# One program instead of three blocks, another routing chain, and register values read ahead of the expert tiles

## The chip, the cores and the metric

The kernel runs on one core of a Trainium2 chip. A core has five engines with a queue of their own: TensorE (PE, matrix products; its weight loads are shown as PEld), VectorE (DVE), ScalarE (ACT), GpSimd (POOL) and SyncE (SP, here only for DMA transfers). They wait for one another by semaphores. The metric is the device time of one execution in microseconds, as a median of runs.

## What is computed

One layer of a decoder trunk over 1024 prompt tokens and 64 sample tokens (8 sequences of 8), each of width 1024. Token mixing and cross-attention come first; the change concerns the third part, a mixture of 16 experts in 4 groups of 4, of which each token uses two of one group:

```
def hierarchical_moe(h, w_group, b_group, w_router, b_router, w_gate, w_up, w_down):
    g_logits = (t @ w_group).astype(jnp.float32) + b_group.astype(jnp.float32)
    g_prob = jax.nn.softmax(g_logits, axis=-1)
    g_idx = jnp.argmax(g_logits, axis=-1)
    g_p = jnp.max(g_prob, axis=-1, keepdims=True)
    ...
    top_v, top_i = lax.top_k(e_sel, TOP_K_INNER)
    top_w = jax.nn.softmax(top_v, axis=-1) * g_p
    ...
    hg = jnp.einsum('td,edf->tef', t, w_gate)
    hu = jnp.einsum('td,edf->tef', t, w_up)
    a = jax.nn.silu(hg) * hu * gates[..., None].astype(t.dtype)
    y = jnp.einsum('tef,efd->td', a, w_down)
```

A root-mean-square norm with gain `g_ffn` stands ahead of it, a residual sum behind it, and a final norm behind that. An expert has a hidden width of 256.

## The kernel before

The tokens lie in nine tiles of 128 rows (`NT = 9`; tiles 0 to 7 are the prompt, tile 8, `TS`, holds the 64 sample rows and padding). Products that need f32 accuracy are made of three products of a high and a low part (`split_product`, L1503 to L1508); the high part is a rounding on ScalarE, the low part (`Wl`, `xTl`, `aTl`, `pTl`) a subtraction on VectorE.

The program consists of three blocks with a barrier of all engines between them.

Block 1 is mixing (`front_stage`) and attention (`attention_stage`). In the attention's last loop over tiles t, PE makes the scores of tile t+1, turns the probabilities of tile t (`turn_probs`) and multiplies them with the folded values (`out`, two halves of 24 products); DVE adds the result to the residual `X` (L995) and counts up `x2_ok`.

Block 2 is `routing_block` (L1202). For each of the nine tiles ScalarE sums squares (L1291), GpSimd makes the factor (L1280, L1283), DVE scales the row (`r_xs`, L1366), PE turns it by eight transposes (L1338), ScalarE copies the turned tile (`r_hT`, L1305), and PE makes 20 logits, 4 for groups and 16 for experts (L1324, L1325), which are copied and turned once more (`r_lgT`, L1295, L1329). SP stores the scaled rows in `h_rows` (three buffers), loads the first three experts' weights (nine transfers of 1 MB, `raw`) and stores `X` in `acc_rows`. Then a chain on DVE follows, in which nearly every step waits for the one before by `step_ok`: it picks the group (`G1`) and the two experts (`H`), makes the gate weights (`wt`), 0/1 rows for each token and choice (`M`, and their sum `Ms`), and has PE count how many tokens of each expert come earlier, within a tile (`before`) and in each tile as a whole (`ones`). From the counts DVE makes each choice's slot: running sums over the tiles (`run`, L1427), tiles per expert and first tile (`tl`, `base`), the slot's tile and row (`rk`, `bk`, `fl`, `rr`, `tt`). It builds one-hot matrices for the row (`r_big`, 18 x 128 columns, L1454) and the tile (`r_A`, with token numbers in one half and weights in the other, L1457 to L1462); 18 products on PE (L1354) turn them into a table of token numbers and of gate values for up to 32 tiles of slots. Meanwhile DVE makes tables for the engines' registers (`TAB`: does an expert start at this tile, where its weights lie, the last tile of each; L1467 to L1489). At the end it writes `idx` (L1496), `gate` and `idx_last`.

Block 3 is `experts_block` (L1512). `tile_steps` goes over the tiles of 128 slots; from the 18th on each is inside a condition, and with these inputs 27 tiles run. For each one GpSimd gathers rows of `h_rows` into `xg` (L1618) and of `acc_rows` into a ring (L1630), PE turns the rows (L1776), ScalarE and DVE split them (L1688, L1728), PE makes gate and up (`gate_up`, 24 products), ScalarE the silu (L1701), DVE the product with the gate value (L1740), PE turns that (`turn_a`, L1798) and multiplies it with the down weights (`down`, 12 products), DVE adds (L1748), GpSimd scatters (L1637). The weights of an expert are three pieces (`raw`, 128 x 2048 each), split at the tile where the expert starts (L1682 on ScalarE, L1723 on DVE). The engines read what they need from `TAB` into registers (`value_load`: `starts` L1551, `started` L1555, `place` L1559, `end` L1563, `tail` L1567, `sums` L1571, `last_slot` L1577). Behind the last tile PE reads two more values and does the last `down`; DVE reads four and adds (L1760); GpSimd waits for the scatter before (L1657) and for that sum (L1659) and issues the last scatter. Then the nine tiles are loaded from `acc_rows`, normed and stored.

## Time and profile before

| | us |
|---|---|
| median of 3 runs (1052.6 to 1054.3) | 1053.1 |
| the profiled execution's own time | 1054.8 |
| its span, first to last instruction | 1053.1 |
| PE busy | 940.9 (89%) |
| PE weight loads busy | 761.5 (72%) |
| DVE busy | 443.0 (42%) |
| ACT busy | 339.7 (32%) |
| POOL busy | 172.5 (16%) |

The profile is one execution seen by the hardware profiler. Times count from its first instruction. Busy shares of the whole span say little here, since the stages have different limits; the rows below are of stretches. An entry in square brackets behind a row is the time that the engine stood idle before it and what it waited for.

### The profile page before, as it was taken

To read this page: it belongs to the slowest core of one execution; us is meant where nothing else is said; L and a number is where in the kernel's file an instruction comes from. 1 tells how busy PE (TensorE), PEld (TensorE's weight loads), DVE (VectorE), ACT (ScalarE), POOL (GpSimd) and SP (SyncE) were. 2 spreads that over 40 slices of the span, in tenths; PEclk is the share of its full clock that TensorE was granted. 3 is DMA by queue.
4 is the path that set the end of the run, shared out by engine and by line. 5 is a ranking of instruction groups with operands and counts; after the bars stand their busy time and mean duration, and the time that the engine had idled before them with its cause. 6 is when DMAs were issued, how large, how long until landed. Compare 5 with 4: busy or idle time off the path is not lost. (4 is left out here: it accounts for less than half of the span.)

```text
span 1053.1 us, 14135 instructions
## 1 busy us (share of the span) xinstructions
PE 940.9 (89%) x4765; PEld 761.5 (72%) x4765; DVE 443.0 (42%) x565; ACT 339.7 (32%) x489; POOL 172.5 (16%) x188
## 2 busy tenths in 40 slices
PE   6996999999999999898999999763798999999960
PEld 5785888888888686466888887653587878787750
DVE  5673212212122124322322222437677786756724
ACT  6762012120121114122221211520555464444403
POOL 0011000000000000000100000400224453534511
PEclk9998999999999999998999999885799999999985
DMA  9892101111013985620000100793378888776328
GB/s 375 354 298 72 47 4 40 40 41 41 1 40 156 367 346 221 260 100 1 1 1 1 31 1 0 251 338 131 95 275 310 324 309 324 255 285 245 119 66 349
DMA packets 41391, 171.47 MB, mean 163 GB/s; under 512 B 8779, under 2 KB 13259, under 8 KB 30810
## 3 DMA queue, kind: packets, MB, share of 16 engines
q1 hardware_dynamic: 29266, 143.16, 36.1%
q0 software_dynamic: 12048, 27.32, 7.4%
q8 instruction: 44, 0.72, 0.3%
q14 instruction: 33, 0.27, 0.1%
HBM read 149.18 MB, written 37.63 MB: 177 GB/s over the span
## 5 line engine op out<-in xcount | busy, mean ns | idle before, releaser
L1723 DVE TENSOR_TENSOR Wl<-raw,Wh x48 | 109.4, 2289 | 64.6 <-ACT Wh L1682 64.6
L1682 ACT CAST Wh<-raw x48 | 91.1, 1910 | 73.6 <-issue 71.7
L1506 PE MATMUL ps<-Wh,e_xTh 128*128 x216 | 87.7, 406 | 7.1 <-issue 5.2
L558 PE MATMUL ps<-f_win_h,f_hTh 128*128 128x512 f32 x216 | 85.9, 398 | 0.6 <-DVE f_hTl L450 0.6
L1508 PE MATMUL ps<-Wh,e_xTl 128*128 x216 | 84.8, 392 | 0.0
L1507 PE MATMUL ps<-Wl,e_xTh 128*128 x216 | 84.8, 392 | 0.0
L560 PE MATMUL ps<-f_win_l,f_hTh 128*128 128x512 f32 x216 | 84.3, 390 | 0.0
L559 PE MATMUL ps<-f_win_h,f_hTl 128*128 128x512 f32 x216 | 84.1, 389 | 0.0
L1637 POOL DMA_INDIRECT acc_rows<-x,idx x26 | 46.6, 1793 | 118.2 <-DVE x L1748 47.6
L1506 PE MATMUL ps<-f_rg_h,f_cTh 128*128 128x512 f32 x144 | 56.7, 394 | 0.0
L1508 PE MATMUL ps<-f_rg_h,f_cTl 128*128 128x512 f32 x144 | 56.2, 390 | 0.0
L1507 PE MATMUL ps<-f_rg_l,f_cTh 128*128 128x512 f32 x144 | 56.1, 390 | 0.0
L1506 PEld LDWEIGHTS ps<-Wh,e_xTh 128*128 128x128 f32 x216 | 40.9, 189 | 19.5 <-issue 11.7
L1506 PE MATMUL ps<-t_WKh,t_hTh 128*128 128x512 f32 x128 | 51.8, 405 | 3.3 <-DVE t_hTl L940 3.3
L1506 PE MATMUL ps<-t_VWh,t_pTh 128*128 128x512 f32 x128 | 50.4, 394 | 2.4 <-DVE t_pTl L984 2.4
L1507 PE MATMUL ps<-t_WKl,t_hTh 128*128 128x512 f32 x128 | 50.9, 397 | 0.0
L1508 PE MATMUL ps<-t_WKh,t_hTl 128*128 128x512 f32 x128 | 50.8, 397 | 0.0
L1507 PE MATMUL ps<-t_VWl,t_pTh 128*128 128x512 f32 x128 | 49.8, 389 | 0.0
L1508 PE MATMUL ps<-t_VWh,t_pTl 128*128 128x512 f32 x128 | 49.8, 389 | 0.0
L517 DVE TENSOR_TENSOR f_xin<-f_xin,ps 128x512 f32<-128x512 f32 x18 | 12.4, 688 | 86.8 <-PE ps L1508 86.8
L267 POOL TENSOR_SCALAR f_st<-f_st 128x1 f32<-128x1 f32 x20 | 4.4, 219 | 270.5 <-ACT f_junk L347 223.3
L1508 PEld LDWEIGHTS ps<-Wh,e_xTl 128*128 128x128 f32 x216 | 40.8, 189 | 8.8
(315 smaller groups left out, 1899.7 us busy)
## 6 DMA issues: line engine op xcount, KB each, us to landing
raw<-in_w_e SPq DMA_DIRECT2D x48, 1024.0 KB, 8.5
t_ring<-in_kc SPq DMA_DIRECT2D x8, 1024.0 KB, 12.3
t_ring<-in_vc SPq DMA_DIRECT2D x8, 1024.0 KB, 8.4
f_win_raw<-in_w_in SPq DMA_DIRECT2D x3, 2048.0 KB, 23.6
f_xin<-in_x SPq DMA_DIRECT2D x9, 512.0 KB, 3.5
x_rows<-f_xin SPq DMA_DIRECT2D x9, 512.0 KB, 2.6
h_rows<-r_xs SPq DMA_DIRECT2D x9, 512.0 KB, 7.7
acc_rows<-x SPq DMA_DIRECT2D x9, 512.0 KB, 13.8
```

Source lines behind the costliest of these rows:

```text
L267: pool.tensor_scalar(st[:, c + 1:c + 2], st[:, c:c + 1], 1.0 / width, EPS, ALU.mult, ALU.add).then_inc(ok, 1)
L517: dve.tensor_tensor(half, half, ps[:, 7 if h == 0 else 5, :], ALU.add).then_inc(x1_ok, 1)
L558: pe.matmul(ps[:, bank, :], hTh[:, c, :], win_h[i][:, c, :], start=(c == 0), stop=False)
L559: pe.matmul(ps[:, bank, :], hTl[:, c, :], win_h[i][:, c, :], start=False, stop=False)
L560: last = pe.matmul(ps[:, bank, :], hTh[:, c, :], win_l[i][:, c, :], start=False, stop=(c == KC - 1))
L1506: pe.matmul(out, xh, wh, start=(n == 0), stop=False)
L1507: pe.matmul(out, xh, wl, start=False, stop=False)
L1508: last = pe.matmul(out, xl, wh, start=False, stop=(n == len(pairs) - 1))
L1637: pool.indirect_dma_start(acc_dram[:, :], bass.IndirectOffsetOnAxis(ap=IDX[:, j:j + 1], axis=0), ring[:, j % 4, :], None, bounds_check=NT ...
L1682: act.copy(Wh[q][:, ds(off, PIECE)], raw[q][:, ds(off, PIECE)]).then_inc(hi_ok[q], 1)
L1723: dve.tensor_tensor(Wl[q][:, ds(off, PIECE)], raw[q][:, ds(off, PIECE)], Wh[q][:, ds(off, PIECE)].bitcast(F32), ALU.subtract).then_inc(lo_ ...
```

## The change

The three blocks become one. `routing_block` is now `routing_stage` and `experts_block` `experts_stage`; both return one program for each engine, which `build` calls behind the attention's. No barrier stands between them; semaphores on single buffers do (`h_st`, `idx_ok`, `routed`, `x2_ok`, `out_ps`, `sc_ps`). The tiles are routed in the order 8, 0, 1, ..., 7 (`ORD`).

Into the attention's last steps go: three sums of squares on ScalarE, the scaling of the first three tiles on DVE, and on PE the turn of the first one. In SP's queue six weight pieces start when the last scores are done, three when the last product is done, and then the nine stores of `X`. The scaled rows are stored from ScalarE's queue. The scaled rows lie in `xg`, which isn't cleared any more.

The chain: logits are read from PSUM directly; the gate weights are computed behind the index; the counts come from ten bf16 products that sum up over earlier tiles (and give the totals in one more group of 16 columns); a slot's position is one number (`pos`), of which the tile is taken by adding and subtracting 1.5 x 2^23; `A` and the one-hot rows are bf16, the latter written by 18 instructions, each releasing one of 18 bf16 products that give the index. The gate values are 18 f32 products of their own (`G`). The register tables are made behind that, in `dve_tables`.

In the experts: ScalarE rounds the first expert's three pieces inside the routing program, DVE subtracts two of them ahead of the tables and the third behind; PE does tile 0 without registers and turns tile 1 behind tile 0's gate and up; DVE reads its four values for the end ahead of the tiles, PE its two in tile 1.

```
+            if t == TS - 1:
+                turn_scaled(pe, 0)
             for n in range(2):
                 out(t, n)
...
+            if t == TS - 1:
+                scaled(dve, 0)
+                scaled(dve, 1)
+            if t == TS:
+                scaled(dve, 2)
             if t >= 1:
                 for h in range(2):
                     dve.wait_ge(out_ps, 2 * (t - 1) + h + 1)
...
+        sp.wait_ge(A_["sc_ps"], 2 * TS)
+        for n in range(RING):
+            for p in (1, 2):
+                if n:
+                    sp.wait_ge(keep["w_ld"][p], 16 * n)
+                load_piece(sp, io, keep, n, p)
+        sp.wait_ge(A_["out_ps"], 2 * TS)
+        for n in range(RING):
+            if n:
+                sp.wait_ge(keep["w_ld"][0], 16 * n)
+            load_piece(sp, io, keep, n, 0)
+        for n, t in enumerate(ORD):
+            sp.wait_ge(A_["x2_ok"], 2 * n + 1)
+            sp.dma_start(acc_dram[t * P:(t + 1) * P, :], X[:, t, :]).then_inc(keep["acc_st"], 16)
...
+            act.copy(hT[n % 2][:, :, :], ps[:, BT(n), :].rearrange("p b (c t) -> p (b c) t", t=P)).then_inc(hT_ok, 1)
+            act.wait_ge(xs_ok, n + 1)
+            act.dma_start(h_dram[ORD[n] * P:(ORD[n] + 1) * P, :], xs[:, n % XG, :]).then_inc(h_st[n % XG], 16)
...
+        pe.matmul(ps[:, 6, 0:(NT + 1) * NE], before_b[:, :], Ms[:, :, :].rearrange("p t e -> p (t e)"), start=True, stop=False)
+        for n in range(NT):
+            last = pe.matmul(ps[:, 6, (n + 1) * NE:(NT + 1) * NE].rearrange("p (t e) -> p t e", e=NE), ones_b[:, :],
+                             Ms[:, n:n + 1, :].to_broadcast([P, NT - n, NE]), start=False, stop=(n == NT - 1))
+        last.then_inc(cnt_ps, 1)
+        pe.wait_ge(nA_ok, 1)
+        pe.wait_ge(pA_ok, 1)
+        for i in range(K2):
+            pe.wait_ge(big_ok, i + 1)
+            last = pe.matmul(ps[:, 7, 0:2 * NTILE].rearrange("p (a n) -> p a n", a=2), big_b[:, i, :], An[:, :, i, :],
+                             start=(i == 0), stop=(i == K2 - 1))
+        last.then_inc(idx_ps, 1)
+        pe.wait_ge(bigf_ok, 1)
+        pe.wait_ge(G_ok, 1)
+        for i in range(K2):
+            last = pe.matmul(ps[:, 4, 0:NTILE], big[:, i, :], G[:, i, :], start=(i == 0), stop=(i == K2 - 1))
+        last.then_inc(gate_ps, 1)
...
+        then(dve.scalar_tensor_tensor(out=R[:, :, :], in0=base_.rearrange("p (o e) -> p o e", o=1).to_broadcast([P, NT, NE]),
+                                      scalar=float(P), in1=rank, op0=ALU.mult, op1=ALU.add))
+        for k in range(2):
+            last = v(MR[:, k, :, 0:NE], M[:, k, :, :], R[:, :, :], ALU.mult)
+        then(last)
+        then(r(pos[:, :], MR[:, :, :, :].rearrange("p k t e -> p (k t) e"), AX_X, ALU.add))
+
+        then(dve.tensor_scalar(ta[:, :], pos[:, :], 0.5 - P / 2, 1.0 / P, ALU.add, ALU.mult))
+        then(dve.tensor_scalar(tb[:, :], ta[:, :], WHOLE, None, ALU.add))
+        then(dve.tensor_scalar(tile[:, :], tb[:, :], -WHOLE, None, ALU.add))
...
+        for i in range(K2):
+            dve.tensor_scalar(big_b[:, i, :], irow_b[:, :], rr[:, i:i + 1], None, ALU.is_equal).then_inc(big_ok, 1)
...
+        rest_of_first(0)
+        rest_of_first(1)
+        rest_of_xT(0, 0)
+        tables(dve)
+        rest_of_first(2)
+        rest_of_piece(1, (0, 1))
...
+        slot, landed, done_by = last_slot(dve), sums(dve, 0), [tail(dve, 1 + h) for h in range(2)]
+        tile_steps(dve, step)
-            tile_steps(dve, step)
-
-            slot, landed, done_by = last_slot(dve), sums(dve, 0), [tail(dve, 1 + h) for h in range(2)]
...
+            gate_up(s, like, *own(s))
+            if s == 0:
+                turn(1, 1)
...
+        last_end = []
+
+        def step_and_end(s, like):
+            step(s, like)
+            if s == 1:
+                last_end.extend((end(pe, NE - 1), tail(pe, 0)))
+        tile_steps(pe, step_and_end)
+        down(NTILE - 1, NE, (NE - 1) % RING * PIECE, last_end[0], [last_end[1]] * 2)
-            tile_steps(pe, step)
-            down(NTILE - 1, NE, (NE - 1) % RING * PIECE, end(pe, NE - 1), [tail(pe, 0)] * 2)
```

In PE's queue the end of the attention and the start of the routing read as follows. `t_VWh` are folded values, `t_E` probabilities, `r_xs` scaled rows (now in `xg`). Before:

```order
L1507 MATMUL ps<-t_VWl_133,t_pTh 128x512
L1508 MATMUL ps<-t_VWh_125,t_pTl 128x512
L1852 UNCONDITIONAL_BRANCH
L1315 UNCONDITIONAL_BRANCH [waits barrier_Pool_Activation_PE_DVE_SP_release]
L1338 MATMUL ps<-ident,r_xs 128x128 [waits r_xs_ok,r_ones_ok,r_c_ld]
L1338 MATMUL ps<-ident,r_xs 128x128 x7
```

and now, first at the turn of the last probabilities, then behind the last product:

```order
L1116 MATMUL ps<-ident,t_E 128x128 [waits t_pT_ok,t_p_ok]
L1116 MATMUL ps<-ident,t_E 128x128 x7
L1375 MATMUL ps<-ident,xg 128x128 [waits r_xs_ok]
L1375 MATMUL ps<-ident,xg 128x128 x7
L1586 MATMUL ps<-t_VWh_127,t_pTh 128x512 [waits t_x2_ok,t_pT_ok]
...
L1588 MATMUL ps<-t_VWh_134,t_pTl 128x512
L1375 MATMUL ps<-ident,xg 128x128 [waits r_xs_ok,r_ones_ok,r_c_ld]
L1375 MATMUL ps<-ident,xg 128x128 x7
L1389 MATMUL ps<-r_hT_157,r_wr 20x128 [waits f_hT_ok]
```

The first turn has moved ahead of the last product of the attention, and the barrier between them is gone. PE's queue from the index product to the first expert tile was, with `r_A` and `r_big` the one-hot matrices:

```order
L1354 MATMUL ps<-r_A,r_big 128x64 [waits r_AB_ok]
L1354 MATMUL ps<-r_A,r_big 128x64 x17
L1204 UNCONDITIONAL_BRANCH
L1769 UNCONDITIONAL_BRANCH [waits barrier_Pool_Activation_PE_DVE_SP_release]
L1776 MATMUL ps<-ident,xg 128x128 [waits e_x_ld0]
L1776 MATMUL ps<-ident,xg 128x128 x7
L1776 MATMUL ps<-ident,xg 128x128 [waits e_xT_ok,e_x_ld1]
L1776 MATMUL ps<-ident,xg 128x128 x7
```

and is now (`r_An` index, `r_G` gate values), up to tile 0's products and then behind them:

```order
L1418 MATMUL ps<-r_An,r_big_b 128x64 [waits r_big_ok,r_pA_ok,r_nA_ok]
L1418 MATMUL ps<-r_An,r_big_b 128x64 [waits r_big_ok] x17
L1424 MATMUL ps<-r_G,r_big 128x32 [waits r_G_ok,r_bigf_ok]
L1424 MATMUL ps<-r_G,r_big 128x32 x17
L1862 MATMUL ps<-ident,xg 128x128 [waits e_x_ld0]
L1862 MATMUL ps<-ident,xg 128x128 x7
L1586 MATMUL ps<-Wh_63,e_xTh_211 128x512 [waits e_lo_ok1,e_lo_ok0,e_xT_ok]
...
L1862 MATMUL ps<-ident,xg 128x128 [waits e_xT_ok,e_x_ld1]
L1862 MATMUL ps<-ident,xg 128x128 x7
L1884 MATMUL ps<-ident,e_sg 128x128 [waits e_a_ok]
```

A second set of products stands ahead of the first turn, and the turn of tile 1 has moved behind tile 0's gate and up. At PE's end, behind the turn of the last gated tile (`e_sg`), stood:

```order
L1581 UNCONDITIONAL_BRANCH
L1563 TENSOR_LOAD tab
L1563 ISA x2
L1567 TENSOR_LOAD tab
L1567 ISA x2
L1506 MATMUL ps<-Wh_4716,e_aTh 128x512 [waits e_y_ok,e_lo_ok2,e_aT_ok]
```

and stands now:

```order
L1884 MATMUL ps<-ident,e_sg 128x128
L1659 UNCONDITIONAL_BRANCH
L1586 MATMUL ps<-Wh_65,e_aTh 128x512 [waits e_y_ok,e_lo_ok2,e_aT_ok]
L1587 MATMUL ps<-Wl_68,e_aTh 128x512
L1588 MATMUL ps<-Wh_65,e_aTl 128x512
```

The two loads have left the place behind the branch.

## Rows read from the trace of the kernel before

**Rows 1.** Windows: busy us of each engine (instructions), clock, DMA share, GB/s
```profile
756.50:1012.50 256.00, 246.74 (x1188) 202.32 (x1188) 182.30 (x175) 126.18 (x123) 106.13 (x73) 1.00 0.71 256
```

**Rows 2.** DVE in order: start us, us, line, operation, out<-in, idle before
```profile
662.54 0.69 DVE L995 TENSOR_TENSOR x<-x,ps 128x512 f32<-128x512 f32 x1 [4.75 <-PE ps L1508]
...
694.97 1.28 DVE L1366 SCALAR_TENSOR_TENSOR r_xs<-x,r_st,r_gffn 128x1024 f32<-128x1024 f32 x1 [10.31 <-DMA h_rows<-r_xs]
702.53 0.31 DVE L1379 COPY r_EL<-ps 128x144 f32<-128x144 f32 x1 [6.28 <-PE ps L1329]
...
711.85 0.29 DVE L1425 COPY r_tot<-ps 128x144 f32<-128x144 f32 x1 [1.45 <-issue]
...
719.99 0.18 DVE L1451 SCALAR_TENSOR_TENSOR r_rr<-r_fl,r_rk 128x18 f32<-128x18 f32 x1
720.08 0.17 DVE L1452 TENSOR_TENSOR r_WTr<-wt,r_tok 128x18 f32<-128x18 f32 x1
...
720.37 2.56 DVE L1454 TENSOR_TENSOR r_big<-r_rr,r_cst 128x2304 f32<-128x2304 f32 x1
...
725.37 0.72 DVE L1467 TENSOR_TENSOR r_te<-r_base,r_cst 128x544 f32<-128x544 f32 x1
...
731.21 0.15 DVE L1489 CAST tab<-r_used 128x1 int32<-128x1 f32 x1
...
734.15 0.18 DVE L1496 CAST idx<-r_none 128x32 int32<-128x32 f32 x1
```

**Rows 3.** PE in order of time, same columns
```profile
651.33 0.50 PE L1506 MATMUL ps<-t_VWh,t_pTh 128*128 128x512 f32 x1 [2.36 <-DVE t_pTl L984]
...
682.19 1.09 PE L1338 MATMUL ps<-ident,r_xs 128*128 128x128 f32 x8
...
685.55 1.09 PE L1338 MATMUL ps<-ident,r_xs 128*128 128x128 f32 x8
...
699.67 1.92 PE L1324 MATMUL ps<-r_hT,r_wr 128*20 128x128 f32 x16
...
725.50 7.94 PE L1354 MATMUL ps<-r_A,r_big 128*128 128x64 f32 x36 [13.71 <-DVE r_A L1462]
740.57 1.97 PE L1776 MATMUL ps<-ident,xg 128*128 128x128 f32 x8 [7.13 <-DMA xg<-h_rows,idx]
...
746.73 0.79 PE L1506 MATMUL ps<-Wh,e_xTh 128*128 x1
...
756.55 0.49 PE L1506 MATMUL ps<-Wh,e_xTh 128*128 x1 [0.35 <-issue]
```

**Rows 4.** POOL and ACT in order of time, same columns
```profile
736.04 1.21 POOL L1618 DMA_INDIRECT xg<-h_rows,idx  x1 [49.61 <-POOLq L1204]
...
748.00 1.28 ACT L1701 ACT_TABLE_LOAD   x1
```

**Rows 5.** Windows, columns as rows 1: index product, product 0, the end
```profile
725.00:730.00 5.00, 4.50 (x21) 4.50 (x22) 4.69 (x16) 0.00 (x0) 0.00 (x0) 0.50 0.01 3
746.00:750.00 4.00, 4.00 (x13) 3.18 (x12) 3.37 (x2) 2.29 (x2) 1.62 (x2) 0.53 0.52 143
1014.00:1018.00 4.00, 0.89 (x2) 0.82 (x3) 0.00 (x0) 0.00 (x0) 0.99 (x1) 0.75 0.37 139
```

**Rows 6.** Transfers of h_rows: from issue to landing
```profile
DMA to landing us min/median/max: 2.6/6.1/13.6
```

**Rows 7.** The end: a register load of PE, its products, GpSimd's marks
```profile
L1563 PEldq TENSOR_LOAD <-tab x1: 298/298/298, 1015.2 to 1015.2; - x1
...
1017.11 0.76 PE L1506 MATMUL ps<-Wh,e_aTh 128*128 128x512 f32 x1 [4.43 <-issue]
...
1019.01 0.19 POOL L1657 TENSOR_TENSOR e_mark<-nhalf 128x1 f32<-128x1 f32 x1 [4.01 <-DMA acc_rows<-x,idx]
...
1023.49 0.19 POOL L1659 TENSOR_TENSOR e_mark<-nhalf 128x1 f32<-128x1 f32 x1 [4.30 <-DVE x L1760]
```

**Rows 8.** The page's costliest groups: busy us, mean ns, idle before
```profile
L1723 DVE TENSOR_TENSOR Wl<-raw,Wh x48 | 109.4, 2289 | 64.6 <-ACT Wh L1682 64.6
```

1095 lines of the change are left out of this document (559 added, 536 removed).

## The prediction

> **What bounds the kernel now.** I read four views. First the windows by stage, then the instructions of TensorE (PE) and of VectorE (DVE) in order of time from the end of the attention to the first expert tile, then the loads of registers and the chain at the end. In the expert loop PE is busy 246.7 of 256.0 us at full clock [rows 1]; the change doesn't touch what a tile computes, so I leave that stretch at its length. Between the last attention product and the second expert tile it is otherwise. The attention's last sum on DVE starts at 662.54 [rows 2], the product of tile 0 at 746.73 and that of tile 1 at 756.55 [rows 3]: 94 us in which PE does two tiles of real work at most. Inside it the reader sees three pieces. Until 702.53 the nine token tiles are turned and give their logits, at 3.36 us a tile (682.19 to 685.55) [rows 2, 3]. From 702.53 to 734.15 a chain of small DVE operations, nearly all waiting for the one before, finds slots; PE only helps twice, and one of these helps is 7.94 us long [rows 2, 3]. From 736.04 the first gather, transposes, splits [rows 3, 4]. Every microsecond there is on the path. The second place is the end: PE waits for registers until 1017.11 [rows 7].
>
> **Part 1, tiles turned earlier.** The first turn (eight transposes) now stands before the last attention product, where PE idles 2.36 us for the split probabilities [rows 3]; it needs 1.09 us [rows 3] and the row it needs is scaled on DVE some 3 us before (DVE has nothing between its attention steps there). Cost nothing; without that gap it would be 1.1 us. Squares of three tiles and three scalings also go under the last product. So PE can go on at 662.3 with tile 1. Eight tiles at 3.36 us, 0.3 us less for the two that turn no logits, end at 688.9; the last logits and their turns take 702.53 - 699.67 = 2.86 us [rows 2, 3]. DVE starts at 691.75 instead of 702.53: **10.8 us gained**. The old first tiles ran at half clock after a pause; the new ones follow a product. The barriers themselves are nothing: by these rows the engines go on after them within a microsecond.
>
> This holds only if the stores of the normalised rows keep pace. Three buffers serve; a store leaves after the copy of its tile (2.2 us after its turn starts) and must land before the scaling (1.3 us) for the turn three tiles later: 3 x 3.36 - 3.5 = 6.5 us. Before, landing took 2.6 to 13.6 us, median 6.1 [rows 6], in one queue with weights, and DVE once waited 10.31 us for it [rows 2]. Now the stores have ScalarE's queue, six of the nine weight pieces have gone during the last product, the other three go one at a time. I take 5 us and no stall. Weighed against this: the Trainium skill, page "DMA: Bandwidth & Descriptors", section "Issuing engines are not separate DMA queues", says that another issuing engine saves only the time of issuing, since all share 16 engines. By that rule alone the waits of before would come back.
>
> That outcome is rival (a), priced from rows.
>
> **Part 2, the shorter chain.** Before, from the first operation to the pair sums it took 702.53 to 711.85 - 1.45 = 710.40, 7.9 us [rows 2]. Out go the two copies, the group's sum and reciprocal, and eight small operations on weights; in comes one sum. At 0.2 to 0.3 us each that leaves 5.2 us. Counting on PE: before, DVE waited 1.45 us for it [rows 2]; now ten short bf16 products in one sum. No row shows bf16; two f32 products took the 1.45, ten products can hardly cost under 0.9 or over 2.2; I take 1.5, as the columns to be streamed are fewer. Then, from counts to slots: compare and sum 0.7, four shifted sums 0.8, rank 0.3, two products and one sum 1.1, three steps for the tile number 0.6, A 0.7, remainder 0.2, An 0.7. Each is the count times the 0.2 us of an 18-column operation, 0.3 us of a 144-column one and 0.7 us of a 544-column one [rows 2]. Sum 5.1. Gone are the nine chained running sums, the four masked products with sums and the comparison by thresholds. Then eighteen one-hot rows instead of one of 2.56 us [rows 2]. Two unchained small operations follow at 0.09 us (719.99, 720.08), one of 144 columns takes 0.31 [rows 2]: 1.6 to 5.6 us for all; at 128 columns in bf16 I take 0.13 each, 2.3, nearer to the unchained pair, since they don't wait for each other. PE multiplies behind them, +0.3. Index products no longer stand in a row of 7.94 us behind A [rows 3]. The chain to the index product is 5.1 + 2.3 + 0.3 = 7.7. The Trainium skill, page "VectorE: DVE Perf Modes", section "The TRN2 errata", says the fixed cost is paid per instruction, about 150 cycles, and advises tiles of 512 elements or more. Eighteen of them would by its figures be an estimate of 3.4 us, 1.1 more than taken.
>
> So: 691.75 + 5.2 + 1.5 + 7.7 = 706.1; five operations to the index 0.95: 707.1, before 734.33 [rows 2]. The gather then starts at about 707.4 and, as before (736.04 to 740.57 [rows 3, 4]), needs 4.5 us: 711.9.
>
> **Part 3, what takes the place.** Gate values are now a second set of eighteen f32 products on PE, queued ahead of the turn of tile 0. They wait for the weights' chain on DVE, 1.75 us after the index: 708.8. They are half as wide, but before PE was loading weights as long as it was multiplying (PEld 4.50 of 5.00 us, 22 loads, clock 0.50 [rows 5]), so width doesn't help: 36 loads at 0.205 are 7.4, the old price 7.94 [rows 3]; I take 7.7. At full clock it would be 3.9, but over the old row the granted clock stayed at half. They end at 716.5, 4.6 us after the gather has landed. Transposes at half clock 1.97 [rows 3], split 2.4, so the product of tile 0 starts at 720.95. I take 7.4 us for it: before it was 7.2, with the clock at 0.53 until 750 [rows 5]; 5.5 if warm, 10.3 if cold throughout. The split of expert 0's first two pieces, two times 2.29 us [rows 8], runs on DVE under the gate products; without that cover it would be 4.6.
>
> Tables for registers (725.37 to 731.4 = 6.0 us, with the index of the last tile 6.5 [rows 2]) go from in front of the gather to under product 0: DVE ends them at 727.4, the product ends at 728.35. Hidden by 1 us. Behind them DVE has the third piece, 2.29 [rows 8], and four register loads for the end. PE turns tile 1 only after product 0: 0.9, split 1.0 on ScalarE and then, in order, the load of the activation table, 1.28 us, which before was hidden under product 0 [rows 4], silu 0.4, gating 0.5, turn of the activation 0.3, turn of tile 2 0.9, two register loads 1.0. From 728.35 that gives 734.8 against 756.55 [rows 3]: **21.8 us gained** at this point, 4.3 fewer than at product 0 (746.73 - 720.95 = 25.8) [rows 3].
>
> **Part 4, the end.** The first of PE's two register loads started at 1015.2 and the products at 1017.11 [rows 7]; with the values at hand they start at 1015.2, 1.9 us earlier. The branch before stays. The clock is 0.75 on average from 1014 to 1018 [rows 5], so it fell about 1016, and some three of the twelve products get the fast clock: 0.9 more, 2.8 in all. A floor: GpSimd's earlier mark, at 1019.01, waits for another scatter, and the last one came at 1023.49 [rows 7], so at most 4.3 can be had. DVE's four loads of the end leave too, but lay under the products.
>
> **Sum.** 21.8 + 2.8 = 24.6 us. The profiled span is 1053.1, its execution 1054.8, the median 1053.1. By the execution's own time: 1030.2; at the median of before, 1.7 lower: **1028.5**.
>
> **The rivals.**
> (a) Stores starve the scalings: for it speak the 10.31 and 13.6 us of before [rows 2, 6], and that nine stores of the accumulator rows now start in the middle of the logits, not after them. If landings take 8.6 us instead of under 6.5, the two rounds lose 2.1 each; if the last round takes the old 10 to 11, more: 5 in all, time 1033.5. Against: two queues, and less weight traffic.
> (b) The gate products run at full clock or product 0 starts warm: 3.9 + 1.9 less, 1022.7. Against it is the half clock of [rows 5] in the same kind of products.
> (c) Slower: the loop loses its lead. Before, DVE and ScalarE had split weights ahead for some 10 us before tile 1; now tables and register loads take that time. If for each of the 15 later experts one split of 2.29 us [rows 8] came late and PE waited for it, the loop would grow by 34.4 us: 1062.9. It decides from 24.6 / 15 = 1.6 us an expert. Against: PE 246.7 of 256.0 busy [rows 1], so the loop takes its weights in time, and the loads are tied to PE's own progress.
> (d) It doesn't do what it says: one program, but each engine still finds its old last waiter (the turn of tile 1 behind attention's sums, say), and no term holds. Then 1053. Against: the new places in the queues show the waits.
>
> **How the numbers follow.** Forecast 0.62, (a) 0.20, (b) 0.13, (c) 0.03, (d) 0.02. Unknown costs around the forecast: one-hot rows -0.7 to +3.3, counting +-0.7, product 0 -1.9 to +2.9, the end -1.5 to +0.9; together some +-4.5: 1024 to 1033. With (a) and (b) the range is 1020.5 to 1037. About 0.2% (2 us) is what a measurement can tell from no change. Faster 0.95, same 0.02, slower 0.03.
>
> **What would show it.** Right: DVE's first logits operation near 692; the cast of the index near 707; gate products near 709 to 717 at clock 0.5; product 0 at 721, product 1 at 735; a load of the activation table after the second split; the last twelve products from 2 us after the branch. (a) shows as DVE waits for the row stores between 665 and 690, (c) as PE waits for split weights in the loop. Wrong would make it above all the gate products (their clock) and the loop's length, if it isn't 256 us from product 1 to its end.

## The result

The changed kernel takes 1038.4 us (median of 1036.7, 1039.6, 1043.0 and 1037.2), the kernel before 1053.7 in the same comparison. The ratio is 0.9861, 95% interval 0.9825 to 0.9897. It is faster, by 15.3 us, where 24.6 were predicted; 1038.4 lies 1.4 us above the range. Run again twice it gave ratios of 0.9866 and 0.9870, so it is worth 14 to 15 us. All its times in the three comparisons lie between 1034.7 and 1044.7. One execution each of silu2 and noendpad (below) took 2161.7 and 1620.2 us and is in no ratio.

Its profiled execution took 1036.7, with a span of 1035.0 against 1053.1. That is 18.1 us: the profile shows one of its best runs. So I read three profiles of it. Each span is cut at eight marks, the starts of: VectorE's (DVE's) last addition of the attention (A), its first logits operation (L), its cast of the index (X), product 1 of TensorE (PE) (P1), the turn of tile 3 (T3), the last e_aTl on DVE (E), the last addition to the last tile (V), the end of the span (S).

| stretch | predicted | before | after, three profiles | mean short of the prediction |
|---|---|---|---|---|
| to A | 662.54 | 662.54 | 660.81, 663.85, 664.82 | 0.6 |
| A to L | 29.21 | 39.99 | 31.38, 32.92, 32.96 | 3.2 |
| L to X | 15.35 | 31.62 | 15.58, 15.57, 15.58 | 0.2 |
| X to P1 | 27.7 | 22.40 | 27.98, 27.95, 27.96 | 0.3 |
| P1 to T3 | 8.5 | 8.50 | 10.34, 10.23, 10.28 | 1.8 |
| T3 to E | 248.07 | 248.07 | 247.91, 248.89, 247.79 | 0.1 |
| E to V | 6.8 | 9.60 | 9.40, 10.20, 9.48 | 2.9 |
| V to S | 30.38 | 30.38 | 31.60, 31.99, 31.13 | 1.2 |
| span | 1028.5 | 1053.1 | 1035.0, 1041.6, 1040.0 | 10.3 |

The predicted column is the prediction's working, cut at these marks. Its 707.1 for X is the end of the cast (it is compared with 734.33); taken as a start it moves 0.2 us between the two rows beside X. The routing (L to X and X to P1) came out as predicted. The missing 10.3 us are in four places: before L, behind P1, behind E and, smaller, ahead of A and behind V.

DVE of the changed kernel in order of time (columns as in rows 2), from the stores of h_rows to the second tile's split and the end:

```profile
667.82 1.28 DVE L1437 SCALAR_TENSOR_TENSOR xg<-x,r_st,r_gffn 128x1024 f32<-128x1024 f32 x1 [5.12 <-DMA h_rows<-xg]
...
675.08 2.52 DVE L1437 SCALAR_TENSOR_TENSOR xg<-x,r_st,r_gffn 128x1024 f32<-128x1024 f32 x2 [4.51 <-DMA h_rows<-xg]
684.57 1.28 DVE L1437 SCALAR_TENSOR_TENSOR xg<-x,r_st,r_gffn 128x1024 f32<-128x1024 f32 x1 [6.97 <-DMA h_rows<-xg]
...
692.19 0.20 DVE L1474 TENSOR_REDUCE r_gmax<-ps 128x9 f32<-128x36 f32 x1 [6.00 <-PE ps L1394]
...
698.46 0.31 DVE L1497 TENSOR_TENSOR r_cmp<-ps,r_cst 128x144 f32<-128x144 f32 x1 [0.31 <-PE ps L1411]
...
707.77 0.18 DVE L1531 CAST idx<-r_none 128x32 int32<-128x32 f32 x1
...
732.02 1.22 DVE L1812 TENSOR_TENSOR e_xTl<-ps,e_xTh 128x1024 fp32r<-128x1024 f32 x1 [1.70 <-ACT e_xTh L1769]
733.17 0.48 DVE L1827 SCALAR_TENSOR_TENSOR e_sg<-e_sg,gate,ps 128x256 f32<-128x256 f32 x1
...
994.00 0.42 DVE L1837 TENSOR_TENSOR e_aTl<-ps,e_aTh 128x256 fp32r<-128x256 f32 x1
...
1003.40 0.69 DVE L1847 TENSOR_TENSOR x<-ps,x 128x512 f32<-128x512 f32 x1 [1.31 <-PE ps L1588]
```

These answer [rows 2]. The first logits operation stands at 692.19 instead of 702.53, the index at 707.77 instead of 734.15. Two waits for a store, 10.31 the longer and 14.9 us in all, have become four, 16.8 us in all, of which the last, 6.97, holds PE for 2.08 us (next rows). PE in order of time, which answers [rows 3, 7]:

```profile
685.91 1.09 PE L1375 MATMUL ps<-ident,xg 128*128 128x128 f32 x8 [2.08 <-DVE xg L1437]
...
709.78 7.86 PE L1424 MATMUL ps<-r_G,r_big 128*128 128x32 f32 x36 [2.89 <-DVE r_G L1541]
717.46 1.95 PE L1862 MATMUL ps<-ident,xg 128*128 128x128 f32 x8
721.77 0.80 PE L1586 MATMUL ps<-Wh,e_xTh 128*128 128x512 f32 x1 [2.36 <-DVE e_xTl L1812]
...
729.35 1.03 PE L1862 MATMUL ps<-ident,xg 128*128 128x128 f32 x8
733.70 0.69 PE L1884 MATMUL ps<-ident,e_sg 128*128 128x128 f32 x2 [3.32 <-DVE e_sg L1827]
734.18 1.92 PE L1862 MATMUL ps<-ident,xg 128*128 128x128 f32 x8
735.75 0.78 PE L1586 MATMUL ps<-Wh,e_xTh 128*128 x1
...
993.18 0.38 PE L1884 MATMUL ps<-ident,e_sg 128*128 128x128 f32 x2
995.94 0.76 PE L1586 MATMUL ps<-Wh,e_aTh 128*128 128x512 f32 x1 [2.38 <-issue]
996.50 0.63 PE L1587 MATMUL ps<-Wl,e_aTh 128*128 128x512 f32 x1
999.11 0.79 PE L1588 MATMUL ps<-Wh,e_aTl 128*128 128x512 f32 x1 [1.98 <-issue]
```

The turn before the pause takes 1.03 us for eight transposes, the one behind it 1.92: full and half clock. At the end one wait of 4.43 [rows 7] has become two, 2.38 and 1.98, and the products still take 0.63 us at first, at half clock. Windows of the changed kernel (columns as in rows 1), the pause with the start of product 1, and the loop, which answers [rows 1]:

```profile
733.50:740.00 6.50, 6.30 (x21) 5.41 (x22) 4.99 (x5) 4.51 (x4) 1.96 (x2) 0.52 0.48 162
```
```profile
737.50:993.50 256.00, 246.54 (x1185) 202.26 (x1184) 179.99 (x174) 123.59 (x121) 102.97 (x74) 1.00 0.71 257
```

The loop is what it was: 246.5 us busy in 256.

**Where runs of one kernel differ.** Over all profiles of both kernels and of the experiments, A lies between 660.8 and 667.7 us. No experiment touches the code ahead of A, and the change only its last products (one turn, three scalings). The windows from 440 to 495 us of the earliest (the changed kernel) and the latest (its variant pad, below) differ in PE's granted clock:

```profile
440.00:495.00 55.00, 50.44 (x270) 32.77 (x269) 16.27 (x24) 14.36 (x23) 2.22 (x6) 1.00 0.24 90
```
```profile
440.00:495.00 55.00, 50.47 (x248) 31.13 (x247) 15.79 (x23) 14.36 (x23) 2.22 (x6) 0.94 0.31 121
```

The kernel before had 0.94 there too. Over the first 660 us the granted clock was 0.98 in the four profiles with the latest A (664.5 to 667.7: again2, bend, hold, pad) and 0.99 in all others (660.8 to 663.9). So A goes with the clock, and the 1.7 us by which it came earlier in the first profile of the changed kernel are most likely luck. Times alone leave some 0.3% open, 3 us. The experiments are read by the marks, of which L to X and X to P1 repeat to a few hundredths (27.95 to 27.98) and A to L and E to V to 1.6 and 0.8 us, and by the ratio where it can tell.

### The profile page after: what moved, and what is told of

Same layout as the page of the kernel before. It is cut to its first block, busy times and chain, and to the rows that moved or that the text cites. A ratio compares the mean times of both kernels' runs of the same rounds, so it can differ in the third digit from the quotient of the medians.

```text
span 1035.0 us, 14111 instructions
## 1 busy us (share of the span) xinstructions
PE 939.0 (91%) x4789; PEld 761.3 (74%) x4789; DVE 438.4 (42%) x563; ACT 342.6 (33%) x494; POOL 167.5 (16%) x188
## 4 chain that ended last, share of the span: by engine, by line
PE 80%; DMA 6%; DVE 6%; issue 3%; ACT 2%; ACTq 1%; DVEq 1%; SPq 1%; POOL 0%; POOLq 0%
PE ps L1586 15%; PE ps L1588 15%; PE ps L1587 15%; PE ps L560 4%; PE ps L562 4%; PE ps L561 4%; PE ps L1043 3%; DMA t_ring<-in_vc 2%; PE ps L1862 2%; PE ps L543 2%; PE ps L588 1%; PE ps L544 1%; PE ps L545 1%; DMA x<-acc_rows 1%; DMA vt_cols<-f_kT 1%
## 5 line engine op out<-in xcount | busy, mean ns | idle before, releaser
L1807 DVE TENSOR_TENSOR Wl<-raw,Wh x45 | 102.6, 2290 | 58.0 <-ACT Wh L1763 57.9
L1763 ACT CAST Wh<-raw x45 | 85.5, 1910 | 43.7 <-issue 42.7
L1586 PE MATMUL ps<-Wh,e_xTh 128*128 (+1 forms) x216 | 88.6, 410 | 9.2 <-issue 5.4
L1587 PE MATMUL ps<-Wl,e_xTh 128*128 (+1 forms) x216 | 85.8, 397 | 0.0
L1588 PE MATMUL ps<-Wh,e_xTl 128*128 (+1 forms) x216 | 85.7, 397 | 0.0
## 6 DMA issues: line engine op xcount, KB each, us to landing
acc_rows<-x SPq DMA_DIRECT2D x9, 512.0 KB, 13.2
```

The source lines that it names most:

```text
L1586: pe.matmul(out, xh, wh, start=(n == 0), stop=False)
L1587: pe.matmul(out, xh, wl, start=False, stop=False)
L1588: last = pe.matmul(out, xl, wh, start=False, stop=(n == len(pairs) - 1))
L1763: act.copy(Wh[q][:, ds(off, PIECE)], raw[q][:, ds(off, PIECE)]).then_inc(hi_ok[q], 1)
L1807: dve.tensor_tensor(Wl[q][:, ds(off, PIECE)], raw[q][:, ds(off, PIECE)], Wh[q][:, ds(off, PIECE)].bitcast(F32), ALU.subtract).then_inc(lo_ ...
```

## Experiments

### The changed kernel again (again, again2)

> The changed kernel once more, nothing altered, to see how far its own times lie apart. Its four times so far lie between 1036.7 and 1043.0 us, with a granted clock of 0.951 in the longest and 0.960 and 0.962 in the two shortest. Theory: the first wide products start at half clock, and what differs from run to run is how long, so a second profile shows the same places (late start of the last scaling, half clock after the turns of tile 0 and behind the pause before the first turn_a) with other lengths; median 1036 to 1040, ratio to before 0.983 to 0.988. Rival: the spread comes from transfers that the merged program starts earlier (stores of h_rows and acc_rows beside the expert weights); then the stall of DVE's last scaling, 7.0 us so far, moves by more than 1.5 us between the two profiles.

Measured: ratio 0.9866 (0.9836 to 0.9897), median 1040.4, 0.4 us above the range given; marks in the table. DVE's last scaling waited 6.96 us and PE 2.00, as before; but behind that wait PE ran at half clock:

```profile
688.86 1.50 PE L1375 MATMUL ps<-ident,xg 128*128 128x128 f32 x8 [2.00 <-DVE xg L1437]
690.29 3.13 PE L1389 MATMUL ps<-r_hT,r_wr 128*20 128x128 f32 x16
```

In the first profile the same two rows took 1.09 and 1.92 us. So the stall repeats, and behind it the clock falls in most profiles, 1.6 us more: of the eleven with a wait of 1.77 to 2.45 us there, in nine. The two that stayed at full clock had waited 2.08 and 2.30 us, so the length of the wait doesn't decide it alone. The rival is out, the theory holds in kind; the half clock is in one more place than it named.

> The changed kernel as it is, a third time, as the standard for the runs beside it: product 1 at 28.0 us behind the index, turn of tile 3 at 38.2 to 38.5, two waits in the last down product (2.2 to 2.4 and 2.0 to 2.9 us), 1038 to 1041 us in the median. What differs between its runs is, by the two profiles so far, the time at which the attention ends (660.8 and 663.9 us, 3.0 of the 6.6 us between their spans), the half clock behind the wait of the last scaling (0 or 1.6 us) and the second wait at the end (2.0 or 2.9 us).

Measured: ratio 0.9870 (0.9838 to 0.9902), median 1042.4. X to P1 27.96, T3 38.24 behind X, waits of 2.18 and 2.34 at the end. All as expected, but that the median is 1.4 us above the range given.

### The registers of the end (bend, noend, noendpad)

bend is the kernel before with this part of the change alone; in noend it is undone in the changed kernel:

```diff
-        slot, landed, done_by = last_slot(dve), sums(dve, 0), [tail(dve, 1 + h) for h in range(2)]
         tile_steps(dve, step)
+        slot, landed, done_by = last_slot(dve), sums(dve, 0), [tail(dve, 1 + h) for h in range(2)]
...
-        tile_steps(pe, step_and_end)
-        down(NTILE - 1, NE, (NE - 1) % RING * PIECE, last_end[0], [last_end[1]] * 2)
+        tile_steps(pe, step)
+        down(NTILE - 1, NE, (NE - 1) % RING * PIECE, end(pe, NE - 1), [tail(pe, 0)] * 2)
```

> The kernel before with one part of the change alone: TensorE reads its two registers for the end in tile 1 and VectorE its four ahead of the tiles. Theory of the prediction: the register reads cost, 2.8 us gained (1.9 from the reads, 0.9 from a clock that doesn't fall), ratio 0.9973. Rival, from the trace after the change: behind the branches over the tiles that don't exist TensorE's instructions come by a transfer of their own (queue 8, 1 packet at 1012.0 us), and a second packet is fetched at 1016.0 us while the register reads wait; without the reads the wait for the second packet comes back between the products: first product 2 us earlier, a new gap of 2 us two products later, 0 to 0.4 us gained, ratio 0.9996 to 1.0.

Measured: E to V 6.09 instead of 9.60 us, the gain of 2.8 that the prediction took and 0.7 more. The first wait is 2.1 us shorter (2.30 for 4.43, 1.9 predicted), and the twelve products run at full clock (0.4 us apiece for 0.63), worth 2.2 us where 0.9 was taken. The second wait that the rival named is there, but it stands eight products in and is short:

```profile
1018.80 0.47 PE L1506 MATMUL ps<-Wh,e_aTh 128*128 128x512 f32 x1 [2.30 <-issue]
...
1021.68 0.50 PE L1508 MATMUL ps<-Wh,e_aTl 128*128 128x512 f32 x1 [0.81 <-issue]
```

Both are wrong in part. The ratio is 1.0007 (0.9983 to 1.0031), which leaves out the 0.9973 of the theory and takes in the rival's. In the profile A came 1.9 us later and T3 to E was 2.2 longer, which hides the 3.5; but the six times don't bear the gain out, so it stands on one profile.

> The changed kernel with that part undone: the registers for the end are read behind the tiles again. Theory of the prediction: 2.8 us slower than the changed kernel. Rival (instructions fetched in two packets): the gap ahead of the last down product goes back to 4.4 us and the gap between its products goes, 0 to 0.4 us slower.

Measured: E to V 11.72 us against 9.40 to 10.20, so 1.5 to 2.3 us slower there; ratio 0.9870 (0.9842 to 0.9899), no difference that the time shows. PE around the wait:

```profile
1000.19 0.77 PE L1586 MATMUL ps<-Wh,e_aTh 128*128 128x512 f32 x1 [4.47 <-issue]
1000.76 0.63 PE L1587 MATMUL ps<-Wl,e_aTh 128*128 128x512 f32 x1
1003.09 0.80 PE L1588 MATMUL ps<-Wh,e_aTl 128*128 128x512 f32 x1 [1.70 <-issue]
```

The old wait is back, 2.1 us longer than without the reads (4.47 for 2.38), and the new one stays: the rival, that one would take the place of the other, is wrong in this form. Reads and second wait are two costs.

### Another place for the last instructions (pad)

```diff
+            if s == NTILE - 1:
+                for _ in range(40):
+                    pe.transpose(ps[:, 6, 0:P], sg[:, 0:P], ident[:, :])
```

> The changed kernel with 40 transposes added to the code of tile 31, which doesn't exist in this data and is never run: they only move the code of the last down product to another place. If the second gap of 2.0 us (two products into the last down product) is an instruction packet that ends there, the code now begins elsewhere in a packet and the gap goes or moves behind the products: 2.0 us shorter from the last e_aTl to VectorE's last addition (9.6 to 7.6 us) and about 2 us faster than the changed kernel. If the gap is something else (a wait for a buffer, the clock), it stays where it is and the time is the same.

Measured: E to V 6.86 us instead of 9.40 to 10.20; ratio 0.9835 (0.9806 to 0.9865), 3 us less than the changed kernel's 0.9866, though the two intervals overlap. PE has one wait in the last products:

```profile
1004.48 0.77 PE L1586 MATMUL ps<-Wh,e_aTh 128*128 128x512 f32 x1 [2.78 <-issue]
1005.05 0.63 PE L1587 MATMUL ps<-Wl,e_aTh 128*128 128x512 f32 x1
```

Instructions that never run gain 2.5 us and more in this stretch. The queues of transfers show why. In the changed kernel a packet of the instruction queue starts between 996.5 and 997.0, where the second wait begins (queue, kind: packets, MB, share of 16 engines):

```profile
q8 instruction: 1, 0.02, 15.2%
```

Another one starts at 993.0 to 993.5, ahead of the first wait. In pad the first comes at 1001.5 to 1002.0 and the second at 1006.0 to 1006.5, behind products that go on without a wait. In the kernel before they came between 1012.0 and 1012.5 and between 1016.0 and 1016.5 us, the second while PE still waited for its registers; in noend at 995.5 to 996.0 and 1000.5 to 1001.0, the second behind the first product. In the eleven profiles with a second wait the products go on 2.3 to 3.1 us behind the start of the second packet. The reading that fits all of them: the code behind the branch begins a few instructions ahead of the end of a packet in the changed kernel, and there the next packet is asked for too late. It lets the products go on 3.2 us after the first of them (995.94 to 999.11), in bend 2.9 us after (1018.80 to 1021.68), so a packet's end two products in costs 2 us and one eight products in 0.8. The Trainium skill, page "Runtime: NRT & Kernel Launch", section "Instruction fetch mechanics", says that instructions come in blocks of 16 KiB (256 of them), fetched in sequence, that crossing a block is mostly hidden, and that a taken branch to a block that isn't there must wait for it. The trace agrees with the wait behind the branch (2.2 to 2.8 us); it adds that the crossing right behind one isn't hidden (2.0 to 2.9 us).

noendpad: the transposes of pad and the reads behind the tiles.

> The changed kernel with the registers for the end read behind the tiles again, and the 40 transposes in the tile that is never run, so that the last down product's instructions come in one packet. Against the kernel with the transposes alone (6.9 us from the last e_aTl to VectorE's last addition, one wait of 2.8 us) this prices the register reads by themselves. Theory (the reads cost what the prediction took, 1.9 us and a clock that falls): one wait of 4.4 to 4.7 us, 8.8 to 9.7 us to the last addition. Rival (the reads run while the packet is fetched, so they cost nothing by themselves): 6.9 to 7.2 us.

Measured: one wait of 3.75 us, 7.87 us from E to V, against 2.78 and 6.86 in pad; ratio 0.9875 (0.9839 to 0.9911). From the first product to V both take 4.5 us, with half of the products at half clock in each. PE's first register load (the second started at 1000.8) and its first product:

```profile
L1641 PEldq TENSOR_LOAD <-tab x1: 298/298/298, 1000.1 to 1000.1; - x1
```
```profile
1001.79 0.47 PE L1586 MATMUL ps<-Wh,e_aTh 128*128 128x512 f32 x1 [3.75 <-issue]
```

The reads themselves took 1.7 us (1000.1 to 1001.8), 1.8 in noend and 1.9 in the kernel before [rows 7], one behind the other and ahead of the products: not hidden. The difference from pad is only 1.0 because PE's first instruction behind the branch came 2.1 us after the last turn here and 2.7 in pad; why is open. Neither side's number for the whole: 0.9 to 1.8 us less than the theory, 0.7 more than the rival.

### The stores in one stage (hold)

```diff
+        for b in range(XG):
+            sp.wait_ge(h_st[b], 16 * (NT // XG))
         for n, t in enumerate(ORD):
             sp.wait_ge(A_["x2_ok"], 2 * n + 1)
```

> The changed kernel, but SyncE starts the nine stores of acc_rows only when all stores of h_rows have landed. So far the h_rows store for which the last scaling waits takes 9.3 us, with acc_rows stores issued beside it from 674 us on; VectorE waits 7.0 us, TensorE 2.0 us, and in the second profile the clock fell to half behind that wait, for another 1.6 us. Theory (the acc_rows stores cause the stall): the store lands in 5 to 7 us, TensorE's wait and the half clock behind it go; from the end of the attention (VectorE's last addition there) to the first logits operation 29.3 us instead of 31.4 to 33.3, 2 to 4 us gained, ratio to before 0.981 to 0.985. Rival (the weight loads cause it, they are issued earlier on the same engine and are still running): 31.4 to 33.3 us stays, nothing gained, and the tile loop may wait for the later acc_rows stores.

Measured: A to L 29.43 us, where the prediction had 29.21 and the changed kernel has 31.38 to 32.96; ratio 0.9838 (0.9816 to 0.9860), within the range given. Time to landing of the nine h_rows stores in the kernel before, in the changed kernel and in hold:

```profile
DMA to landing us min/median/max: 2.6/7.7/13.6
```
```profile
DMA to landing us min/median/max: 4.3/6.9/9.3
```
```profile
DMA to landing us min/median/max: 2.6/5.2/7.3
```

The stores of acc_rows took 13.2 us in the median and take 4.9 now, and still land before the first gather needs them: X to P1 is 27.96. PE in hold turns the last tile 3.57 us after the one before (the cadence is 3.36), at full clock:

```profile
684.25 1.09 PE L1377 MATMUL ps<-ident,xg 128*128 128x128 f32 x8
...
687.82 1.09 PE L1377 MATMUL ps<-ident,xg 128*128 128x128 f32 x8
688.84 1.92 PE L1391 MATMUL ps<-r_hT,r_wr 128*20 128x128 f32 x16
```

The theory holds, the rival falls. (Its E to V was 10.54 us, a little above that of the changed kernel.)

### The pause ahead of turn_a (warm)

```diff
             if s == 0:
                 turn(1, 1)
+                for _ in range(28):
+                    pe.transpose(ps[:, 7, 0:P], ident[:, :], ident[:, :])
```

> The changed kernel with work added: 28 transposes of the identity matrix into a bank that nobody reads, behind the turn of tile 1, about 3.3 us by the 0.12 us that one of a turn's eight took at full clock, in the pause in which TensorE waits for the gating of tile 0. Theory (the pause lets the clock fall): turn 2 takes 1.06 instead of 1.92 us, the wide products behind it 0.23 instead of 0.43 us each, and from the first turn_a to the turn of tile 3 it is 10 instead of 12.4 us: 2.0 to 2.5 us gained for the work added. Rival (the half clock is left over from the gate products, or comes back whatever TensorE does): nothing gained, and turn_a is up to 1 us later where the transposes run at half clock: 0 to 1 us slower.

Measured: P1 to T3 8.51 us, as before the change (8.50), instead of 10.2 to 10.3; T3 comes 36.27 us behind X instead of 38.2. Ratio 0.9797 (0.9773 to 0.9821), since the transposes also moved the end's code, with E to V 6.91. PE:

```profile
734.12 3.22 PE L1912 MATMUL ps<-ident 128*128 128x128 f32 x28
737.71 0.44 PE L1884 MATMUL ps<-ident,e_sg 128*128 128x128 f32 x2 [0.38 <-DVE e_sg L1827]
737.99 1.04 PE L1862 MATMUL ps<-ident,xg 128*128 128x128 f32 x8
```

The theory holds. Useless work in the pause makes the kernel faster: the pause's price was the clock behind it.

### The table load, and what hid it (silu, silu2)

```diff
+        act.activation(mark[:, 2:3], nhalf[:, :], ACT.Silu)
         round_xT(0, 0)
```

> The changed kernel with a Silu of one column on ScalarE ahead of its first expert work, so that the table of that function (ACT_TABLE_LOAD, 1.28 us, between product 0 and the gating) is loaded while ScalarE waits for the turn of tile 0. Theory: the load stands in the chain, so turn_a of tile 0 and product 1 come 1.3 us earlier (index ready to product 1: 26.7 instead of 28.0 us); the pause of TensorE is 2.0 instead of 3.3 us, and if 2 us is short enough for the clock another 2 us come ahead of the turn of tile 3. Rival (the subtraction for tile 1 on VectorE, done at 733.2 us in the profiled run, sets the gating): nothing gained until then, at most 0.3 us.

Measured: X to P1 27.96 us, nothing gained; ratio 0.9868 (0.9841 to 0.9895). The rival is right. DVE in silu:

```profile
736.23 1.23 DVE L1813 TENSOR_TENSOR e_xTl<-ps,e_xTh 128x1024 fp32r<-128x1024 f32 x1 [1.70 <-ACT e_xTh L1769]
737.37 0.47 DVE L1828 SCALAR_TENSOR_TENSOR e_sg<-e_sg,gate,ps 128x256 f32<-128x256 f32 x1
```

The index was cast at 711.99, so the subtraction starts 24.24 us behind it, as in each of the eight profiles with DVE's four register reads ahead of the tiles and the gate products in one piece. The profile names ScalarE as releaser, whose half had ended at 735.36, 0.9 us earlier. In noend, without the reads there, it starts at 23.77. silu2 moves those reads into tile 3:

```diff
-        slot, landed, done_by = last_slot(dve), sums(dve, 0), [tail(dve, 1 + h) for h in range(2)]
-        tile_steps(dve, step)
+        def step_and_end(s, like):
+            step(s, like)
+            if s == 3:
+                last_end.extend((last_slot(dve), sums(dve, 0), [tail(dve, 1 + h) for h in range(2)]))
+        tile_steps(dve, step_and_end)
```

> The changed kernel with two edits: the Silu table early (which alone gained nothing), and VectorE's four register reads for the end moved from ahead of the tiles into tile 3. In every kernel with these reads ahead of the tiles, VectorE's subtraction for tile 1 begins 24.24 us behind the index, 4.0 us behind the end of the tables, with or without other work between; where the reads stand behind the tiles it begins at 23.8. Theory (two chains of nearly one length, table load and Silu to 25.2 us, register reads and subtraction to 25.4, hid each other): with both shortened the subtraction begins at 23.4 to 23.5 us, when ScalarE's half is done, the gating at 24.6 to 24.8 and product 1 at 27.2 to 27.4 instead of 28.0 us behind the index: 0.6 to 0.8 us gained. Rival: something else (the third weight piece, the branch itself) holds the subtraction: 24.24 and 28.0 us stay.

Measured: subtraction at 23.68, product 1 at 27.39, T3 at 36.38 us behind X instead of 38.2: 0.6 us at product 1 and 1.9 in all, since the pause is shorter and the clock comes back sooner. Ratio 0.9840 (0.9806 to 0.9874). The reads moved alone gave nothing either (noend: product 1 at 28.05). So two chains of one length stood side by side, and the change itself had put the second there.

### The way to product 1 (gsplit, early1)

gsplit cuts the gate products in three. It also copies the gate values just ahead of the first gating, so that DVE's tables no longer wait for them (not shown here):

```diff
-        for i in range(K2):
+        for i in range(a, b):
             last = pe.matmul(ps[:, 4, 0:NTILE], big[:, i, :], G[:, i, :], start=(i == 0), stop=(i == K2 - 1))
...
         turn(0, 0)
+        keep["gate_sums"](pe, 9, 14)
...
             if s == 0:
+                keep["gate_sums"](pe, 14, 2 * NT)
                 turn(1, 1)
```

> The changed kernel with the gate products cut in three: 9 of 18 pairs where they stand, 5 behind the turn of tile 0 (while ScalarE and VectorE split it), 4 behind product 0; the column of gates is copied just ahead of the first gating, and the tables no longer wait for it. So the gather of tile 0 and the split hide half of their 7.9 us. Theory (TensorE's own order sets product 0): turn 0 at 6.2 us behind the index instead of 9.7, product 0 at 10.5 to 11 us instead of 14.0, product 1 about 3 us earlier (25 instead of 28.0 us). Rival (the gather of tile 0, 4.4 to 5.2 us to landing, or VectorE's tables are next): product 0 comes 3 us earlier, but VectorE's tables and the third weight piece (6.4 and 2.3 us) then end last, and product 1 gains 1 us or less.

Measured: turn 0 at 5.85, product 0 at 10.16, product 1 at 25.20 us behind X; ratio 0.9838 (0.9811 to 0.9866). The theory holds to 0.4 us. PE:

```profile
710.54 4.02 PE L1427 MATMUL ps<-r_G,r_big 128*128 128x32 f32 x18 [2.89 <-DVE r_G L1546]
714.37 1.95 PE L1871 MATMUL ps<-ident,xg 128*128 128x128 f32 x8
716.11 2.18 PE L1427 MATMUL ps<-r_G,r_big 128*128 128x32 f32 x10
718.68 0.79 PE L1589 MATMUL ps<-Wh,e_xTh 128*128 128x512 f32 x1 [0.39 <-DVE e_xTl L1817]
```

early1 turns tile 1 ahead of product 0 and tile 2 behind it, and takes DVE's third weight piece after the gating:

```diff
         turn(0, 0)
+        turn(1, 1)
...
-            if 1 <= s < NTILE - 1:
+            if 2 <= s < NTILE - 1:
...
             if s == 0:
-                turn(1, 1)
+                turn(2, 2)
```

> The changed kernel with another order around product 0: TensorE turns tile 1 ahead of product 0 (as the kernel before did) and tile 2 behind it, ahead of turn_a; VectorE takes the rest of the third weight piece after the gating of tile 0 instead of ahead of the subtraction for tile 1. In the runs so far that subtraction ended last: it began 1.7 us after ScalarE's half, 24.2 us behind the index, with or without the table load of 1.28 us ahead of the Silu. Theory: the turn costs 2.0 us at half clock ahead of product 0 (16.0 instead of 14.0 us behind the index), product 0 ends at 22.4, the subtraction for tile 1 at about 23.3, turn_a at 24.7, product 1 at 25.2 instead of 28.0, and as TensorE waits under 1.5 us in one piece the clock stays: the turn of tile 3 at 33.5 instead of 38.2 us behind the index, 4.5 us gained; from tile 3 to the last e_aTl 247 to 250 us as everywhere. Rival: product 0 is only moved behind by the turn and VectorE's tables are then last; product 1 at 27 us or later.

Measured: product 0 at 15.68, product 1 at 27.63, T3 at 36.64 us behind X; ratio 0.9849 (0.9824 to 0.9875). Of 2.8 us expected at product 1 only 0.3 came, as the rival said: DVE's subtraction again started 24.24 us behind X. But its tables had ended at 20.2, and nothing but register reads and a branch lay between. This is what pointed to the reads. PE waited 2.90 us there and turned tile 2 at half clock (1.94 us).

### All together (best, bestall, best2)

best is gsplit, early1 and silu in one.

> The three changes ahead of product 1 together: the order of early1, the gate products in three parts, the Silu table early. Theory (their gains add up where they hide different things): index to product 0 about 12.2 us, its end at about 19.5, product 1 at 21.8 (28.0 in the changed kernel), turn of tile 3 at about 30.5 instead of 38.2: 7 to 8 us gained on the changed kernel. Rival: with TensorE's chain short, VectorE is last (two weight rests 4.5, subtraction 1.2, tables 6.4, branch 1.7, subtraction 1.2 us), or ScalarE waits for the expert weights: product 1 at 24 us or later, 4 us gained.

Measured: product 0 at 11.84, product 1 at 23.78, T3 at 34.91 us behind X; ratio 0.9803 (0.9781 to 0.9826). 4.2 us at product 1 and 3.3 at T3, where 7 to 8 were expected: the rival is nearer. bestall adds hold and pad.

> All that the runs so far showed to help: best, with the acc_rows stores held until the h_rows stores have landed (end of the attention to first logits operation 29.4 us instead of 31.4 to 33.3, measured) and the 40 transposes in the tile that is never run (last e_aTl to last addition 6.9 us instead of 9.4 to 10.2, measured in two kernels whose code was moved). Theory (independent places, they add up): 5 to 6 us less than best, 1025 to 1028 us, ratio to before 0.970 to 0.976. Rival: the acc_rows stores, now started near 690 us, are still running beside the gathers, which come 6 us earlier than in the kernel where the hold was measured; then gathers land later or the first additions of the tile loop wait, and at most 3 us come.

Measured: 1028.1 us against 1056.5, ratio 0.9733 (0.9709 to 0.9758); A to L 29.3, E to V 4.90, X to P1 23.78. The theory holds, at the upper end of its range, 7.4 us below best where it had 5 to 6. best2 moves DVE's reads as silu2 does.

> The kernel with all that helped, and VectorE's four register reads for the end moved into tile 3. There they were the longest wait ahead of tile 1: 4.0 us from the end of VectorE's tables to its subtraction for tile 1. Theory: the subtraction begins as soon as ScalarE's half is done (18.2 instead of 20.2 us behind the index), the turn of tile 2 follows product 0 and the rest of the gate products without a wait, product 1 at 21.8 to 22.3 instead of 23.8 us, TensorE's clock doesn't fall there, turn of tile 3 at 30.5 to 31 instead of 33.0 us: 2 us less than that kernel, 1025 to 1027 us. Rival: ScalarE's gating inputs or the weight pieces are next: product 1 at 23 us or later, 1 us or less.

Measured: product 1 at 21.81 and T3 at 30.32 us behind X (23.78 and 32.95 in bestall). The subtraction for tile 1 in bestall, then in best2:

```profile
727.88 1.23 DVE L1820 TENSOR_TENSOR e_xTl<-ps,e_xTh 128x1024 fp32r<-128x1024 f32 x1 [4.03 <-issue]
```
```profile
725.27 1.23 DVE L1820 TENSOR_TENSOR e_xTl<-ps,e_xTh 128x1024 fp32r<-128x1024 f32 x1 [2.02 <-ACT e_xTh L1776]
```

The 4.03 us of issue were five register reads, 0.6 to 1.0 us each, and a branch. The profiled span is 1022.3 instead of 1026.3. The time is 1028.1 in the median, ratio 0.9758 (0.9729 to 0.9787), against 1054.5: by the times bestall and best2 can't be told apart (1025 to 1027 was expected), by the marks the second is 2.6 us ahead at T3. Of that E to V gave 1.6 back, 6.52 us for 4.90: behind a wait of 2.2 us in both, the last products ran at full clock in bestall and at half in best2. Both beat the changed kernel by 10 us and more.

## The prediction, step by step

**Part 1, 10.8 us for tiles turned earlier: right but for one term, which failed.** The cadence of 3.36 us, the turn in the old gap and the counting of tiles hold, since hold gives 29.43 for 29.21. What failed is "I take 5 us and no stall". The stores landed in 6.9 us in the median, 9.3 at most, against 6.5 allowed. The row that it rested on misled: the median of 6.1 [rows 6] mixes the nine stores with 28 gathers, and the stores alone had taken 7.7 in the median before the change, more than allowed. The last of the two rounds stalled PE for 2.0 us, and behind it the clock fell in two of three profiles, 1.6 us more. This is rival (a) in part: one round of two, and its cause was among those named there, the stores of acc_rows in the middle of the logits. The page's rule in the Trainium skill, "DMA: Bandwidth & Descriptors", section "Issuing engines are not separate DMA queues", had been weighed and put aside; the trace agrees with it: stores issued by SyncE delayed those issued by ScalarE. The rival missed that a short stall is priced twice, by its length and by the clock.

**Part 2, the routing: right.** L to X was 15.6 us for 15.35. Inside, two errors nearly met: counting took 1.1 instead of 1.5, and the eighteen one-hot rows 3.0 instead of 2.3. The group of the changed kernel (busy us, mean ns | idle before):

```profile
L1522 DVE TENSOR_SCALAR r_big_b<-r_irow_b,r_rr 128x128 bf16<-128x128 bf16 x18 | 3.0, 249 | 0.0
```

That is 0.17 us apiece. The estimate from the page "VectorE: DVE Perf Modes" of the Trainium skill, section "The TRN2 errata", was 3.4; the trace lies between it and the row I had taken.

**Part 3, product 0 and 1: right in size, partly by luck.** Gate products 7.86 us at half clock (7.7 predicted), product 0 14.0 us behind the index (13.85), product 1 28.0 (27.7). Rival (b) is out. Behind product 0 two errors met: the two register loads, 1.0 us in the sum, lay under the turn of tile 2 and cost nothing, while turn_a and that turn ran at half clock and took 2.05 us for 1.2. (And 25.8 less 21.8 is 4.0, not the 4.3 that the prediction gives; nothing rests on it.) I had the table load in the chain, and it was; but DVE's four register loads, which I named and gave no price, had made a second chain of the same length, so taking the load away gained nothing. What failed is the step after: the loop's start was left as before. PE's pause of 3.3 us ahead of turn_a, which my own times imply, let the clock fall, and P1 to T3 took 10.3 us for 8.5: 1.8 us given back, shown by warm.

**The loop, left at its length: right.** T3 to E 247.8 to 248.9 us for 248.1. Rival (c) is out.

**Part 4, the end, 2.8 us: the term came to nothing.** E to V was 9.40 to 10.20 us for 9.60. The price of the reads was right: the wait behind the branch fell from 4.43 to 2.2 to 2.4 us, 2.1 for the 1.9 taken. What failed is the step behind them: the prediction let the twelve products follow without a gap and, late, at full clock. The changed kernel's code has another place, its last products meet a packet's end two products in, and that costs 2.0 to 2.9 us (pad takes it away); with that wait most products stayed at half clock, and the 0.9 us for a clock that falls later didn't come. In the kernel before, the same edit alone gave 3.5 us in this stretch of the one profile (bend), though not in the times.

**The rest of the difference.** V to S was 1.2 us longer in these three profiles. In the twelve other variants of the changed kernel it was 30.1 to 32.4; in the two of the kernel before it was 30.4 and 31.0; I take it as scatter, which no run tests. A came 0.6 us later in the mean. The sum of the table's last column is 10.3 us: 3.2 + 1.8 + 2.9 are explained and shown by experiments, 0.5 are small sizes, 1.9 scatter.

Rival (d) is out. The range missed by 1.4 us because its cases were added around a likeliest one that left three costs at nothing: the stall with the clock behind it, the clock behind the pause ahead of turn_a, and the second wait at the end. All three fell on the slow side.
